# Experts ranked by token count into wide and small jobs that run in pairs, in a two-layer decoder trunk on one core

## The reference

```python
logits = (x @ w_router).astype(jnp.float32)
top_vals, top_idx = lax.top_k(logits, TOP_K)          # TOP_K = 2 of 8 experts
top_w = jax.nn.softmax(top_vals, axis=-1)
...
for e in range(N_EXPERTS):
    out = out + gates[..., e:e + 1].astype(x.dtype) * swiglu(x, w_gate[e], w_up[e], w_down[e])
```

## Time and profile before

| | |
|---|---|
| time, three executions | 1434.13 to 1434.95 us, median 1434.71 |
| span of the profiled execution | 1433.4 us (the median is 1.3 us above it) |
| PE, PEld, DVE, ACT busy | 99%, 83%, 80%, 67% |
| granted TensorE clock, mean | 0.999 of full speed |
| mixture of experts, from its first matmul to its last | 450.05 to about 1397 us |
| DMA in the expert stage | 373 to 395 GB/s per 100 us |

### The profile page before, as it was taken

One profiled execution on the slowest core, in us unless ns is written; L12 is line 12 of the kernel. 1 busy time (PEld: TensorE's weight loads), 2 busy tenths in 40 slices (PEclk: granted clock), 3 DMA queues, 4 the chain that ended last, 5 costly groups with the idle time before them and its releaser, 6 DMA issues.

```text
span 1433.4 us, 19865 instructions
## 1 busy us (share of the span) xinstructions
PE 1418.3 (99%) x7061; PEld 1195.2 (83%) x7061; DVE 1148.5 (80%) x987; ACT 966.5 (67%) x895; POOL 88.5 (6%) x96
## 2 busy tenths in 40 slices
PE   9999999999999999999999999999999999999997
PEld 8988888889997888888888888888888888888885
DVE  5776544567658889888988988988898898898996
ACT  5555434346547777777777877777777787777775
POOL 2000000000004750000000000000000000002000
PEclk9999999999999999999999999999999999999999
DMA  9758655564543999999999999999999999999990
GB/s 321 251 176 318 221 180 193 188 235 148 171 153 145 399 395 394 395 394 382 369 393 371 374 394 380 358 397 392 363 389 393 379 360 394 377 351 397 396 368 30
DMA packets 197798, 454.59 MB, mean 317 GB/s; under 512 B 7481, under 2 KB 28997, under 8 KB 197758
## 3 DMA queue, kind: packets, MB, share of 16 engines
q1 hardware_dynamic: 190944, 429.94, 81.7%
q0 software_dynamic: 5040, 17.92, 3.4%
q10 hardware_dynamic: 1774, 6.17, 1.1%
HBM read 439.30 MB, written 14.70 MB: 317 GB/s over the span
## 4 chain that ended last, share of the span: by engine, by line
PE 96%; DVE 2%; ACT 1%; DMA 0%; issue 0%; POOL 0%; DVEq 0%; ACTq 0%; POOLq 0%
PE bank L1525 21%; PE bank L991 15%; PE bank L1506 14%; PE bank L1510 14%; PE bank L1513 14%; PE bank L1025 5%; PE bank L1299 4%; PE bank L1492 2%; PE bank L1186 1%; PE bank L1091 1%; ACT w_hi L565 1%; PE bank L1111 0%; DMA work<-in_o_norm_ple 0%; DVE w_lo L1599 0%; PE bank L1473 0%; PE bank L1141 0%
## 5 line engine op out<-in xcount | busy, mean ns | idle before, releaser
L1599 DVE TENSOR_TENSOR w_lo<-raw,w_hi 128x2048 fp32r<-128x2048 f32 x406 | 926.5, 2291 | 208.5 <-ACT w_hi L565 207.2
L565 ACT ACTIVATE w_hi<-raw 128x2048 fp32r<-128x2048 f32 x406 | 779.7, 1921 | 343.5 <-PE bank L1513 145.5
L1506 PE MATMUL bank<-w_hi,x_hi 128*128 128x512 f32 x896 | 244.8, 395 | 0.0
L1510 PE MATMUL bank<-w_hi,x_lo 128*128 128x512 f32 x896 | 240.1, 390 | 0.0
L1513 PE MATMUL bank<-w_lo,x_hi 128*128 128x512 f32 x896 | 239.7, 389 | 0.0
L1510 PEld LDWEIGHTS bank<-w_hi,x_lo 128*128 128x128 f32 x896 | 168.3, 188 | 36.0
L1513 PEld LDWEIGHTS bank<-w_lo,x_hi 128*128 128x128 f32 x896 | 168.2, 188 | 35.2 <-DVE w_lo L1599 0.2
L1506 PEld LDWEIGHTS bank<-w_hi,x_hi 128*128 128x128 f32 x896 | 164.2, 188 | 30.6
L1525 PE MATMUL bank<-w_hi,m_lo 128*128 128x512 f32 x448 | 121.2, 390 | 0.0
L1525 PE MATMUL bank<-w_lo,m_hi 128*128 128x512 f32 x448 | 121.0, 389 | 0.0
L1525 PE MATMUL bank<-w_hi,m_hi 128*128 128x512 f32 x448 | 120.6, 391 | 0.0
(11 more groups left out here) (277 smaller groups left out, 1347.6 us busy)
## 6 DMA issues: line engine op xcount, KB each, us to landing
raw<-in_o_exp_gate SPq DMA_DIRECT2D x112, 1024.0 KB, 7.4
raw<-in_o_exp_up SPq DMA_DIRECT2D x112, 1024.0 KB, 8.0
raw<-in_o_exp_down SPq DMA_DIRECT2D x112, 1024.0 KB, 7.8
raw<-in_o_w_qkv SPq DMA_DIRECT2D x12, 1024.0 KB, 5.1
raw<-in_e_ffn_gate SPq DMA_DIRECT2D x11, 1024.0 KB, 5.2
raw<-in_e_ffn_up SPq DMA_DIRECT2D x11, 1024.0 KB, 5.2
raw<-in_e_ffn_down SPq DMA_DIRECT2D x11, 1024.0 KB, 5.0
raw<-in_e_w_in SPq DMA_DIRECT2D x9, 1024.0 KB, 16.6
```

The lines of the kernel that those rows point to most:

```text
L565: act.activation(w_hi[:, slot % SPLIT], raw[:, slot], ACT.Copy).then_inc(hi_made, 1)
L1506: pe.matmul(dst, x_hi[:, c + kk, 0:P], hi[:, kk], start=(c, kk) == (0, 0), stop=False)
L1510: pe.matmul(dst, x_lo[:, c + kk, 0:P], hi[:, kk], start=False, stop=False)
L1599: ve.tensor_tensor(w_lo[:, slot % SPLIT], raw[:, slot], w_hi[:, slot % SPLIT], ALU.subtract).then_inc(lo_made, 1)
```

## The change

Expert 0 is always wide. The other seven are ranked by their token counts on the chip (`rank_counts`, on DVE); ranks 0 to 2 are wide too, and ranks 3 to 6 are small, with at most 64 rows. A wide job and a small job run as a pair (a "duo") of 7 steps of 12 tiles. An expert with more tokens than its room (128 or 64) gets an extra duo of 84 tiles, of which `EXTRA` = 4 are provided for.

A small job's stationary operand `x_two` holds 64 high columns and 64 low ones side by side, so that two passes (with `w_hi` and with `w_lo`) give high x high, low x high, high x low and also low x low. Its gate and up results come out as a high half and a low half, which 8 matmuls against `stacked` (two identity matrices one above the other) add and turn at once (`fold_small`). It costs 8 matmuls of 512 columns a tile. Two copies by ACT (`gate_copy`, `up_copy`), a silu, a product and a split on 256 columns are new in each step. The result of a small job is folded when it is stored (`fold_y`). SP's load order within a step is wide gate and up, small down, small gate and up, wide down. The first small tiles can't be issued before the ranking is done (`ids_ready`).

```diff
+                    gate_up(wide, b, 0, j, b)
+                    down(small, b + (-1), 4, j, b)
+                    gate_up(small, b, 6, j, b)
+                    down(wide, b, 10, j, b)
+            gate_up(0, 0, 2, None, None)
+            down(0, 0, 6, None, None)
+            sp.wait_ge(ids_ready, 1)
+            gate_up(sp.value_load(job_int[0:1, MOST:MOST + 1], min_val=0, max_val=EXPERTS - 1), 0, 8, None, None)
+            last = last_duo(sp)
+            with sp.Fori(0, last) as j:
+                wide, small = wide_of(j), small_of(j)
+                blocks(wide, small, j)
                 sp.wait_ge(jobs_ready, 1)
-                with sp.Fori(EXPERTS - 1, last) as j:
-                    e = expert_of(j)
-                    blocks(e, j)
-                    first(expert_of(j + 1), j, 6 * BLOCKS - 2)
-                    rest(e, j, 6 * BLOCKS + 2)
-            sp.wait_ge(jobs_ready, 1)
-            e = expert_of(last)
-            blocks(e, last)
-            rest(e, last, 6 * BLOCKS - 2)
...
+            def block(b, j, turn_next=False, first=False, placing=False):
+                st(0, j, b)
+                silu_small(j, b)
+                st(1, j, b)
+                high_small(j, b)
+                silu_wide(j, b)
+                st(2, j, b)
+                if first:
+                    gathered_small(j + 1)
+                    act.wait_ge(y_stored, 32 * j + 32)
+                    y_wide(j, tile_at(11, j, BLOCKS - 1))
+                st(3, j, b)
+                if first:
                     act.wait_ge(y_made, 2 * j + 2)
                     act.dma_start(y_dram[bass.ds(j * P, P), :], y_sb).then_inc(y_stored, 16)
-                st(-1, j, b)
-                act.wait_ge(e_hid_made, hid)
-                silu_of()
-                hidT_of(hid)
-                st(0, j, b)
-                st(1, j, b)
-            gathered_first(0)
+                st(4, j, b)
+                st(5, j, b)
+                turned_wide(j, b)
+                if turn_next:
+                    gathered(0, j + 1)
+                if placing:
+                    act.wait_ge(pickT_ready, 1)
+                    act.activation(place, bank[5][:, :], ACT.Copy).then_inc(place_made, 1)
+                if first:
+                    for half in range(2):
+                        act.activation(y_under[:, half * HALF:(half + 1) * HALF], bank[2 + half][SMALL:P, :], ACT.Copy)\
+                            .then_inc(y_under_made, 1)
+                st(6, j, b)
+                st(7, j, b)
...
+            y_wide(last, tile_at(11, last, BLOCKS - 1))
+            silu_small(last, BLOCKS)
+            high_small(last, BLOCKS)
+            st(0, last, BLOCKS)
             for half in range(2):
-                y_half(last, half, at(6 * BLOCKS - 1, last))
+                act.wait_ge(tile_used, tile_at(1, last, BLOCKS) + 1)
+                act.activation(y_sb[:, half * HALF:(half + 1) * HALF], bank[2 + half][:, :], ACT.Copy).then_inc(y_made, 1)
...
+            def fold_small(j, b):
+                pe.wait_ge(s_copied, 2 * step_no(j, b, 0))
+                for f, src in enumerate((gate_s, up_s)):
+                    for c in range(4):
+                        at = (4 * f + c) * SMALL
+                        mm = pe.matmul(bank[5][:, at:at + SMALL], src[:, c * P:(c + 1) * P], stacked[:, :], start=True, stop=True)
+                mm.then_inc(fold_ready, 1)
+            def wide_tile(i0, i, j, b, rows=None):
...
+            def small_tile(i0, i, j, b):
+                hi, lo = w_tile(MOE_T - 2 + i0 + i, HALF)
+                dst, c = bank[i // 2][:, :], 4 * (i % 2)
+                wait_high(tile_at(i0 + i, j, b))
+                for kk in range(4):
+                    pe.matmul(dst, x_two[:, c + kk, :], hi[:, kk], start=(c, kk) == (0, 0), stop=False)
+                wait_tile(tile_at(i0 + i, j, b))
+                for kk in range(4):
+                    mm = pe.matmul(dst, x_two[:, c + kk, :], lo[:, kk], start=False, stop=(c, kk) == (4, 3))
+                mm.then_inc(tile_used, 1)
...
+            def step(b, j, start=False, turn_next=False, first=False, placing=False, stop=False):
+                rows = j + 1 if first else None
+                pe.wait_ge(s_copied, 2 * step_no(j, b, 0) - 1)
+                wide_tile(0, 0, j, b, rows)
+                fold_small(j, b)
+                wide_tile(0, 1, j, b, rows)
+                if first:
+                    pe.wait_ge(xg_loaded, 32 * j + 32)
+                wide_tile(0, 2, j, b)
+                if first:
+                    turn_small()
+                wide_tile(0, 3, j, b)
+                small_down(4, j, b, start=start, stop=first)
+                if first:
+                    pe.wait_ge(xg_lo_made, 3 * j + 6)
+                turn_wide(j, b)
+                if turn_next:
+                    turn_rows(0, j + 1)
+                if placing:
+                    pe.wait_ge(pick_made, 4 * TT)
+                    for q in range(2):
+                        for t in range(TT):
+                            mm = pe.transpose(bank[5][:, (2 * q + t) * P:(2 * q + t + 1) * P], pick_g[:, q, t], ident)
+                    mm.then_inc(pickT_ready, 1)
+                if first:
+                    pe.wait_ge(xg_hi_made, 3 * j + 6)
+                for i in range(4):
+                    small_tile(6, i, j, b)
+                if turn_next:
+                    pe.wait_ge(hidT_lo_made, step_no(j, b))
+                    turn_rows(1, j + 1)
+                if first:
+                    pe.wait_ge(y_made, 2 * j + 2)
+                wide_down(10, j, b, start=first, stop=stop)
             proj(1, (0, 1))
             gather_first()
             proj(1, (2, 3))
             pe.wait_ge(proj_made, 2)
-            gate_up(0, rows=0)
+            for i in range(4):
+                wide_tile(2, i, None, None, rows=0)
+            gather_small()
...
+            step(BLOCKS - 1, last, stop=True)
+            fold_small(last, BLOCKS)
+            scatter_wide(last)
+            small_down(0, last, BLOCKS, stop=True)
+            scatter_small(last)
...
+            def rank_counts():
+                ve.memset(job_int[:, :], 0)
+                link(ve.memset(erank[:, 0:1], -1.0))
+                mine = count[:, 1:].unsqueeze(2).broadcast_to((P, O, O))
+                other = count[:, 1:].unsqueeze(1).broadcast_to((P, O, O))
+                ve.tensor_tensor(more, other, mine, ALU.is_gt)
+                link(ve.tensor_tensor(same, other, mine, ALU.is_equal))
+                link(ve.tensor_tensor(same, same, before[:, 1:, 1:], ALU.mult))
+                link(ve.tensor_tensor(more, more, same, ALU.add))
+                link(ve.tensor_reduce(erank[:, 1:], more, AX, ALU.add))
+                link(ve.tensor_tensor(by_rank, erank[:, 1:].unsqueeze(1).broadcast_to((P, O, O)),
+                                      eidx[:, 0:O].unsqueeze(2).broadcast_to((P, O, O)), ALU.is_equal))
+                ve.tensor_tensor(rank_ids, by_rank, eidx[:, 1:].unsqueeze(1).broadcast_to((P, O, O)), ALU.mult)
+                link(ve.tensor_tensor(small_terms, pos1[:, :, 1:], by_rank[:, WIDE_RANKS].unsqueeze(1).broadcast_to((P, TT, O)), ALU.mult))
+                ve.tensor_reduce(ids, rank_ids, AX, ALU.add)
+                link(ve.tensor_reduce(small_pos, small_terms, AX, ALU.add))
+                ve.tensor_copy(job_int[:, 1:DUOS], ids[0:1, 0:WIDE_RANKS])
+                ve.tensor_copy(job_int[:, MOST:MOST + DUOS], ids[0:1, WIDE_RANKS:]).then_inc(ids_ready, 1)
+                for t in range(TT):
+                    ve.tensor_scalar(pick_s[:, t], iota[:, 0:SMALL], small_pos[:, t:t + 1], -1.0, ALU.subtract, ALU.is_equal)                        .then_inc(pick_made, 1)
...
+            def block(b, j, turn_next=False, first=False):
                 lo(0, j, b)
-                hidden_of(b, j)
+                hidden_small(j, b)
+                lo(1, j, b)
+                low_small(j, b)
+                lo(2, j, b)
+                hidden_wide(j, b)
+                if first:
+                    gathered_small(j + 1)
+                for i in range(3, 6):
+                    lo(i, j, b)
+                low_wide(j, b)
+                if turn_next:
+                    gathered(0, j + 1)
+                for i in range(6, 9):
+                    lo(i, j, b)
+                if first:
+                    fold_y(j)
+                lo(9, j, b)
+                if turn_next:
+                    gathered(1, j + 1)
+                lo(10, j, b)
+                lo(11, j, b)
             split(OUT1_T + 2 + SPLIT)
-            gathered_first(0)
-            share_routes()
-            gathered_first(1)
+            gathered(0)
+            rank_counts()
+            gathered(1)
...
+            lo(2)
+            share_routes()
+            lo(3)
+            lo(4)
+            hidden_wide(None, None)
+            gathered_small()
+            lo(5)
+            low_wide(None, None)
```

(17 more changed lines are left out.)

603 lines of the change are left out of this document (347 added, 256 removed).

## The result

The changed kernel takes 1417.97 us (median, 1417.33 to 1418.58) against 1434.83 for the kernel before, measured beside it: a ratio of 0.9885, with a 95% interval of 0.9873 to 0.9897. Its profiled execution spans 1416.2 us at a granted clock of 0.992. The forecast was 1411.0, in a range of 1398 to 1428; of the 23.7 us that it promised, 16.9 came.

The account below looks back on a forecast made before the run. The DMA was to replace PE as the bound: tile 15 landing at 488, plus 851 for tiles and 22 for other traffic, plus 12.1 and 36.4 for the end, gave a 1409.5 us span, 1411 with 1.3 added; range 1398 to 1428.

Parts of the forecast that it names:

- The bound and the step: Expert stage: the DMA becomes the bound, at 31.9 us for a step of 12 tiles, where PE took 33.56.
- PE's step: PE's work in a step of 12 tiles after the change: 28.6 us, at most 29.8.
- The cover where duos meet: Where duos meet: 6 us of slot slack hides some 6 us of extra DVE work, costed at nothing.
- its 22 us: Other traffic on the DMA engines (scatter, final gather, rows read, results stored): 8.9 MB at 412 GB/s, 22 us.
- The opening: Before the full load queue: DVE frees tile 9's slot at 482.7 us; tile 15 is issued then and lands at 488.
- From there by bytes: After tile 15: 320 tiles take 851 us, other traffic 22, so the last expert tile lands at 1361 us.
- The end: Behind the last expert landing: the placing comes 12.1 us later, and the rest takes 36.4 us.
- The in-order waits: Rival, 12%: small instructions waiting in DVE's queue add to each step; at 0.5 us a step, 14 us: 1425.
- the slower rival: Rival, 9%: DVE's queue lengthens each step, slower than before from 0.85 us a step; at 1.9 us, 1464.
- The DMA gives more with a full queue: Rival, 5%: the DMA rate rises and DVE bounds the step at 30.2 to 30.6 us, 39 less: 1372.
- The clock: Rival, 2%: PE's pauses in the small half drop its clock to 1.2 GHz, 6 us a step: 1579.

Follow-up runs that it names:

- rows4k: The changed kernel with gate and up tiles loaded from the down weights in one 4 KB row a partition, same bytes, other weights: 1387.81 us.
- down8k: The changed kernel with each down tile read in one row of 8 KB a partition instead of two of 4 KB, result kept: 1410.06 us.
- quarter_low: The changed kernel with one of the four matmuls by the weights' low parts left in each small gate and up tile: 1417.42 us.
- opening: The changed kernel with small rows gathered after the second wide tile and taken out earlier, and the wide hidden product before two tiles' low parts: 1415.15 us.
- tail: The changed kernel with the last small fold, silu, high part, product and low part moved ahead of other work behind the last expert tiles: 1414.32 us.

## Why the prediction came out as it did

- *The bound and the step* (DMA, 8 x 2.71 + 4 x 2.56 = 31.9 us): right, 31.93 measured. That it is the DMA and not a coincidence is shown by `rows4k`, `down8k` and `quarter_low`: rows alone move the time by 30 and 8 us, 336 matmuls fewer by nothing.
- *PE's step* (28.6, at most 29.8 us): 29.5. The fold was the mis-sized term: 16 instructions and 1.89 us where I took 8 and 0.9. It had no effect, since PE had 2.4 us to spare. PE's share is 94.5% instead of the 90% forecast; 29.5 of 31.9 us are 92%, and where the rest comes from is not shown.
- *The cover where duos meet, at nothing*: right. By the landings the two steps of the first meeting take 68.3 us (677.8 to 746.1), 4.4 more than two plain ones. In this stretch the queues other than the weights' hold the DMA engines for 3.4 + 2.9 = 6.3% of the time, which is 4.3 us:

```profile
q0 software_dynamic: 224, 0.79, 3.4%
q10 hardware_dynamic: 224, 0.79, 2.9%
```

So the extra time is bytes, which the sum had in its 22 us, and the engines' extra work is covered. The last meeting, with the final gather, takes 72.0 us, 8.1 more than two plain steps, and these queues hold the engines for 8.8 + 2.7 = 11.5% of it, 8.3 us.
- *The opening* (tile 15 issued at 482.7): its row in the queue's own timeline is at 485.1, 2.4 late. Up to the hidden rows' low part the sum held: the gathering took 3.68 us instead of 1.9 but ended only 0.6 late (464.6 against 464.0), and the low part was ready at 470.8, before the 471.7 of the forecast. The step that failed is "From there DVE runs at one split each 2.3 us": DVE stood 6.57 us for ACT, and ACT 5.60 us for PE, which at the 1.2 GHz level took 5.3 us for the 12 matmuls from 469.94 to 475.19, where 12 take 2.7. The sum had nothing for this wait, nor for the clock. `opening` takes out PE's long wait and the 1.2 GHz stretch (not the length of the gathering, still 3.68 us), and 2.8 us of the time.
- *From there by bytes* (last expert tile lands at 1361): 1364.8, 3.8 late, of which 2.4 is the opening. Tile 15 needed 9.5 us to land and not 5.1, because 1.5 MB of the scatter, which the sum had put behind it, were moved between 485 and 494.5 us; from its landing the rest took 870.3 us instead of 873. So 1.4 is left between errors that go both ways, and I have not taken it apart; 15.96 instead of 15.95 for six tiles makes 0.5 of it.
- *The end* (placing 12.1 us behind the landing): 14.8. The failed step is "two copies (+5.7) and itself (+6.0); product, high and low end at +7.8": a row addition stood ahead of the product on DVE, and the low part ended at +9.4 (1373.85 + 0.42). From there to the placing it was 5.5 us, where the sum had 4.3; 0.5 of this is PE, still at the wide result's placing at 1.2 GHz (1374.76 against 1374.27). `tail` takes 4.0 of the whole back. The rest of the end was 1416.2 - 1379.8 = 36.4, as forecast.
- 2.4 + 1.4 + 2.7 = 6.5, of the 6.7 between the spans (1416.2 against 1409.5). All three go the same way, and the forecast's gain was too large by 40% (23.7 against 16.9); it is the range that held them.
- *The rivals.* The in-order waits do not add to the step: they are the next bound, at 31.04 us with the DMA out of the way, so the cover was 0.9 us a step, less than the 1.5 that 30.4 would have left. From there the slower rival's 32.75 is 1.7 away; it did not come. "The DMA gives more with a full queue" is refused by 394 GB/s over 800 us. The clock did fall to the lower level now and then (below), without a price in the steps, but with one at the opening and a small one at the end, for which the sum had no term.

Weighed against the Trainium skill: DMA: Bandwidth & Descriptors ("Why small descriptors are slow (HBM only)") puts the fixed overhead at some 3 cycles a packet and 32 bytes of metadata a descriptor. As an estimate from its figures (32 bytes a cycle, each row one packet and one descriptor), a 2 KB row would cost 68 cycles and a 4 KB row 132, so that two short rows take 3% longer than a long one. The runs show 2.71 against 2.56, 6%, twice that; the measurement decides.

## What to carry to other kernels

When a change frees the busiest engine, sum the transfers' time by their own row lengths first: here 5% of slack in the DMA turned a saving of 4.1 us a step (33.6 - 29.5) into 1.6 (33.56 - 31.93). A load queue that waits for slots is no proof that the engine freeing them is the bound; look at the DMA share and at the time to landing (7.4 to 8.0 us before by the page, 11.4 to 11.6 after), and test it with an edit that changes only the rows. Once the transfers are the bound, their rows (8 us), the order ahead of the first full queue (3 us) and the order behind the last landing (4 us) are what still paid here.
